# One state-space stage instead of two: tables loaded during the scan, leaving products moved ahead of a last chunk

## What is computed

```python
def _ssm_mixer(hn, ...):
    proj = hn @ w_in                      # 1024 -> 2048
    u, z = proj[..., :SSM_WIDTH], proj[..., SSM_WIDTH:]
    ug = u.reshape(bsz, s, 64, 16)        # 64 groups of 16 channels, 64 complex states each
    y_fwd = _ssm_direction(ug, ...)       # h[t] = abar * h[t-1] + bb @ u[t];  y[t] = Re(c @ h[t])
    y_bwd = flip(_ssm_direction(flip(ug), ...))
    y = y_fwd + y_bwd + d * u
    gl = jax.nn.gelu(y)
    y = gl * jax.nn.sigmoid(gl @ w_glu + b_glu) * jax.nn.silu(z)
    return y @ w_out
```

## Time and profile before

| | us |
|---|---|
| three runs | 2629.58, 2631.95, 2637.1 (median 2631.95) |
| profiled execution | 2628.88 |
| its span, first to last instruction | 2627.0 |
| PE busy | 2325.1 (89%) |
| VectorE busy | 1185.6 (45%) |

### The profile page before, as it was taken

One profiled execution on the slowest core, in us unless ns is written; L12 is line 12 of the kernel. 1 busy time (PEld: TensorE's weight loads), 2 busy tenths in 40 slices (PEclk: granted clock), 3 DMA queues, 4 the chain that ended last, 5 costly groups with the idle time before them and its releaser, 6 DMA issues. The chain is left out here.

```text
span 2627.0 us, 38336 instructions
## 1 busy us (share of the span) xinstructions
PE 2325.1 (89%) x13896; PEld 1865.8 (71%) x13896; DVE 1185.6 (45%) x2668; ACT 886.2 (34%) x2256; POOL 841.2 (32%) x1283
## 2 busy tenths in 40 slices
PE   4999999999999999999999999398799980558888
PEld 3777777777777777777777777277788760457767
DVE  5242443443353353353353353343325999435434
ACT  4233434333433433333333333232433210133221
POOL 1715655555565465466111111010111110211200
PEclk9999999999999999999999999599899995778989
DMA  4212221322222222222221220254554420874333
GB/s 143 60 51 61 60 80 51 84 74 56 74 67 73 66 75 73 66 83 65 64 63 45 47 63 21 65 185 155 202 169 150 144 93 0 213 208 154 136 138 120
DMA packets 191828, 249.69 MB, mean 95 GB/s; under 512 B 86176, under 2 KB 140320, under 8 KB 189472
## 3 DMA queue, kind: packets, MB, share of 16 engines
q1 hardware_dynamic: 191648, 247.30, 31.8%
HBM read 153.23 MB, written 62.55 MB: 82 GB/s over the span
## 5 line engine op out<-in xcount | busy, mean ns | idle before, releaser
L1066 PE MATMUL att_pj<-hT_hi,att_wh 128*128 128x512 f32 (+1 forms) x1920 | 710.0, 370 | 10.8 <-DVE att_wl L848 10.8
L1066 PE MATMUL att_pj<-hT_hi,att_wl 128*128 128x512 f32 (+1 forms) x1920 | 683.8, 356 | 0.0
L1066 PE MATMUL att_pj<-hT_lo,att_wh 128*128 128x512 f32 (+1 forms) x1920 | 682.7, 356 | 0.0
L704 POOL TENSOR_TENSOR att_sw<-att_sw,att_rope 128x1280 f32<-128x1280 f32 x48 | 201.5, 4198 | 762.9 <-DMA att_sw<-att_t 762.8
L1066 PEld LDWEIGHTS att_pj<-hT_hi,att_wh 128*128 128x128 f32 x1920 | 364.5, 190 | 58.5 <-DVE att_wl L848 11.4
L860 DVE CUSTOM_DVE_ANT_0 att_sm<-att_sc,att_mask 128x128 f32<-128x128 f32 (+2 forms) x480 | 152.4, 355 | 561.6 <-PE att_sc L982 560.4
L1066 PEld LDWEIGHTS att_pj<-hT_hi,att_wl 128*128 128x128 f32 x1920 | 363.6, 189 | 53.0
L1066 PEld LDWEIGHTS att_pj<-hT_lo,att_wh 128*128 128x128 f32 x1920 | 364.9, 190 | 45.5
L730 ACT ACTIVATE att_pr<-att_sm,att_stats 128x128 f32<-128x128 f32 (+2 forms) x480 | 215.0, 449 | 434.1 <-PE att_tr L992 313.0
L772 ACT COPY att_t<-att_pj 128x512 f32<-128x512 f32 (+1 forms) x216 | 111.3, 515 | 377.9 <-PE att_pj L1066 377.7
L879 DVE TENSOR_TENSOR att_t<-att_t,att_rope 128x1280 f32<-128x1280 f32 x48 | 71.8, 1495 | 201.8 <-DMA att_sw<-att_t 201.8
(11 more groups left out here) (224 smaller groups left out, 3835.7 us busy)
## 6 DMA issues: line engine op xcount, KB each, us to landing
att_raw<-in_w_att_dram SPq DMA_DIRECT2D x80, 512.0 KB, 3.8
att_sw<-att_t SPq DMA_DIRECT2D x192, 160.0 KB, 2.9
f_scratch<-att_ft SPq DMA_DIRECT2D x32, 256.0 KB, 2.3
e_scratch<-att_place SPq DMA_DIRECT2D x8, 1024.0 KB, 4.6
front_raw<-in_w_ssm_dram SPq DMA_DIRECT2D x16, 512.0 KB, 6.4
front_f<-f_scratch SPq DMA_DIRECT2D x16, 512.0 KB, 5.1
front_f<-e_scratch SPq DMA_DIRECT2D x16, 512.0 KB, 3.6
back_e<-e_scratch SPq DMA_DIRECT2D x8, 1024.0 KB, 7.5
```

The source lines that it names most:

```text
L704: pool.tensor_tensor(sw[:], sw[:], rope[:, 1], ALU.mult).then_inc(sin_done, 1)
L1066: last = pe.matmul(pj[:, c % 3, 0:n], w[:, k % 2, kt], h[:, kt, lo:lo + n], start=(r == 0), stop=(r == CHUNK_MMS - 1))
```

## The change

Front and back become one block, `ssm_stage`. The projection's tiles (`hh`, `hl`, `raw`, `wh`, `wl`, f) give their memory to `e` (seven of eight batches), `near` (all taps), `u2` and `yb`, so the loads of these wait for the last projection product (`done` at 3*NT) and no longer for the end of the scan. PE makes the local products of the first 8 of 24 joints (a joint is 3, 3 or 2 groups of a batch) as soon as they are loaded, into all 8 PSUM banks; after the scan the entering products of joint after joint follow, with the local products of a later joint between them. ACT takes over the forward entering copies from POOL and applies gelu to a whole joint. `states` has no extra column for the zero state (160 instead of 162 columns a row), the scan takes 127 steps (31 for both sequences, 96 for the prompt), and the first column is cleared by DVE ahead of it. In the front part the leaving products of batch n-1 and ACT's copies of them (one instruction a group) go ahead of the third chunk of tile n, and no longer behind it.

```diff
@@ SP
+            sp.wait_ge(k_stored, 16 * HALVES)
+            sp.wait_ge(done, 3 * NT)
+            near_load(0)
+            u_again(0)
+            u_again(1)
+            for b in range(2):
+                e_load(b)
+            near_load(1)
+            near_load(2)
+            for b in range(2, E_BUFS):
+                e_load(b)
+            sp.wait_ge(stored, U_STORED)
+            u_again(2)
+            u_again(3)
+            for b in range(NB):
+                if b + 4 < NB:
+                    u_again(b + 4)
+                sp.wait_ge(y_out, PARTS * (b + 1))
+                for t in range(L):
+                    sp.dma_start(y_scratch[b, :, t].rearrange("(g c) n -> c g n", c=SC),
+                                 yb[t * SC:(t + 1) * SC, b % 2]).then_inc(y_stored[b % 2], 16)
+                if b + E_BUFS < NB:
+                    e_load(b + E_BUFS)
@@ ACT
                 for c, (lo, cnt) in enumerate(CHUNKS):
+                    if c == len(CHUNKS) - 1 and 1 <= n <= NB:
+                        for g in range(GB * (n - 1), GB * n):
+                            act.wait_ge(left, g + 1)
+                            act.copy(states[0:64, g, :, 1:NC], part(g, slice(0, 64))[:, :, 0:NC - 1]).then_inc(fwd, 1)
                     act.wait_ge(done, 3 * n + c + 1)
...
+            def entering(j):
+                if j >= 2:
+                    act.wait_ge(y_done, j - 1)
+                g = joint_groups(j)
+                act.copy(en[0:64, j % 2, 0:len(g)], states[0:64, g[0]:g[-1] + 1]).then_inc(enter_f, 1)
...
+            act.wait_ge(step, 4 * STEPS_ALL + 1)
+            entering(0)
+            entering(1)
+            for j in range(JOINTS):
+                b, g = j // PARTS, joint_groups(j)
+                act.wait_ge(y_done, j + 1)
+                if b >= 2 and j % PARTS == 0:
+                    act.wait_ge(y_stored[b % 2], 16 * L * (b // 2))
+                act.activation(yb[:, b % 2, g[0] % GB:g[-1] % GB + 1],
+                               py[:, j % BANKS, 0:len(g) * NC].rearrange("p (g n) -> p g n", n=NC),
+                               ACT.Gelu_apprx_tanh).then_inc(y_out, 1)
+                if j + 2 < JOINTS:
+                    entering(j + 2)
@@ DVE
-                prev = st[:, :, :, bass.ds(c, n, step=PC + 1)]
-                cur = st[:, :, :, bass.ds(c + 1, n, step=PC + 1)]
+                prev = st[:, :, :, bass.ds(c, n, step=PC)]
+                cur = st[:, :, :, bass.ds(c + 1, n, step=PC)]
...
-            with dve.Fori(0, SCH // TURN) as q:
+            with dve.Fori(0, STEPS_BOTH // TURN) as q:
                 for j in range(TURN):
                     scan_step(TURN * q + j, 2)
+            for c in range(STEPS_BOTH // TURN * TURN, STEPS_BOTH):
+                scan_step(c, 2)
@@ PE
                 for c, (lo, cnt) in enumerate(CHUNKS):
+                    if c == len(CHUNKS) - 1 and 1 <= n <= NB:
+                        leaving(n - 1)
...
-                if 1 <= n <= NB:
-                    leaving(n - 1)
...
+            pe.wait_ge(out, 3 * NT)
+            pe.wait_ge(k_out, 2 * HALVES)
+            for j in range(BANKS):
+                near_part(j)
+            for j in range(JOINTS):
...
+                pe.wait_ge(enter_f, j + 1)
+                pe.wait_ge(enter_b, 2 * (j + 1))
...
+                last.then_inc(y_done, 1)
+                if j >= 1 and j - 1 + BANKS < JOINTS:
+                    pe.wait_ge(y_out, j)
+                    near_part(j - 1 + BANKS)
```

## The result

| | before | after |
|---|---|---|
| median of the runs, us | 2632.44 | 2601.31 |
| lowest to highest, us | 2629.58 to 2637.10 | 2600.31 to 2608.68 |
| profiled execution, us | 2628.88 | 2602.16 |
| its span, us | 2627.0 | 2600.3 |
| waits of PE for u ahead of the leaving products, us | none | 10.7, in 8 waits |

The ratio is 0.9886, interval 0.9863 to 0.9909: 1.1% faster. Four runs of each stand behind it.

A forecast was written before the change was run, and what follows sets the result against it. An end-to-end chain of projection with leaving products, scan and back stage was taken as the bound. From 2628.9 us, -35.3 + 10.7 - 2.3 gave 2602; 3 us more for a median made 2605, range 2588 to 2620.

The forecast's parts named there:

- the three large steps: Against the profiled 2628.9 us: back stage after the scan -35.3, front part ahead of the scan +10.7, scan -2.3; sum 2602.
- Behind the scan: Scan's end to the next stage: 57.4 us in place of 92.7, a gain of 35.3 (30 to 37).
- 46.2 + 1.7 + 1 + 1: Back stage, us: PE's entering and local products 46.2, clock 1.7, ACT in the last joints 1, waits for stores 1.
- the lower clock: Back stage: PE, idle ahead of the scan's end, starts at 1.2 GHz before going to 2.4, costing 1.7 us.
- the waits that I had given 2 us: Back stage: ACT about tied with PE in the last joints, 1 us (0 to 3); gelu waiting for stores, 1 (0 to 4).
- lockstep: Rival, back stage: copy, gelu and products of a joint follow each other; +25 us at worst, half likelier: 2617; chance 0.09.
- lasting lower clock: Rival, back stage: PE stays at 1.2 GHz through the joints, 46.2 us become 92, total 2650; chance 0.04.
- Leaving products ahead: Front part: PE waits 1.7 us for u in 8 batches, 13.6; one third chunk given back, -2.87; net +10.7 us.
- The scan: Scan on VectorE: one step of both sequences gone, 2.32 us; slowing by loads beside it taken as 0.
- The pitch: Scan: rows of `states` at 640 instead of 648 bytes, costed at nothing.
- The rival that a pitch of 640 bytes makes elements dearer: Scan instructions: 126 us hang on it; from 25 us slower than before, at half 2668; chance 0.04.
- The loads: Taps, u and e moved behind the last projection product: 12.8 MB at 245 GB/s, 52 us, hidden in PE's 98 us idle.

## Why the prediction was right, step by step

The forecast was 2605 us, the median is 2601.3, and the signs and sizes of the three large steps hold. On the profiled executions: +11.6 ahead of the scan (10.7 predicted), -3.2 in it (-2.3), -35.2 behind it (-35.3). Together -26.8; the spans differ by 26.7. The sum of the prediction was 2602 for a profiled execution, and 2602.16 was measured. This is closer than the terms deserve: the front part cost 0.9 us more than foreseen, and the scan gave 0.9 more. The 3.7 us between forecast and median come from the 3 us added to get from an execution to a median: after the change the median lies 0.9 us below the profiled execution.

**Behind the scan**, 57.5 us against 57.4 predicted. The same kernel's second profile has 58.9 us here, and those of the kernels that change only the front part 56.6 to 57.6, so agreement to 1 us is what the profiles can show. The first entering product comes 1.2 us after the scan (1.1). From there to PE's end, 2254.11 to 2303.95, is 49.8 us, where I had 46.2 + 1.7 + 1 + 1 = 49.9. Inside, the terms shifted: the lower clock cost 5.99 - 3.42 = 2.6 us and not 1.7, while the waits that I had given 2 us came to the 0.49 for an entering copy at 2299.37; none is for the stores of y. The last gelu at 2303.99 and the stores take 6.45 us (6.4). Rivals: no lockstep, since PE is busy 49.3 of 57.5 us; no lasting lower clock, since the stretch has a granted clock of 0.92. That the early loads are the cause is shown by holding them back (112.6 us), and the share of the early local products by holding those back (65.1).

**Leaving products ahead.** The mechanism is shown by four runs: put back, 11 us are gained; in the kernel before alone, 9 are lost; with u landing 1.8 us sooner, the waits end; made only for the last batch, the front part is 2.9 us shorter than with none ahead. The term itself was not as I had it: 8 waits of 1.7 us were foreseen, 13.6, and they sum to 10.7, 1.34 each. The landing is as foreseen (median 5.7 us), but the load is issued on average 5.65 us after its batch's first store, where it was 6.01 before: three of the eight took 6.5, 6.5 and 7.3 us then, one takes 6.5 now. This is about the 0.36 us that each wait fell short; why these few are longer is not shown. Two things that I had not costed fill the gap. PE's period from the first to the second batch, with a wait of 1.04 us, is 1.28 us longer than before (19.43 against 18.15), so a restart costs 0.24 beyond its wait; the other periods give the same 0.24 or 0.25, 1.9 for eight. And the batch behind the longest wait, 2.08 us, ran 6.29 us instead of 4.61, at a lower granted clock. The stretches are the first 4.6 us of the first, third and seventh batch:

```profile
1880.07:1884.67 4.60, 4.60 (x34) 4.60 (x35) 3.67 (x14) 2.92 (x7) 0.00 (x0) 1.00 0.02 6
1919.98:1924.58 4.60, 4.60 (x22) 4.60 (x23) 2.32 (x9) 1.76 (x5) 0.00 (x0) 0.64 0.04 14
2000.12:2004.72 4.60, 4.59 (x34) 4.60 (x35) 3.75 (x14) 2.92 (x7) 0.00 (x0) 1.00 0.01 4
```

10.7 + 1.9 + 1.7 - 2.87 = 11.4 of the 11.6 measured; the total was near by errors that offset each other, which is luck. In the kernel before with the reordering alone, where no batch ran slow, 10.0 + 1.9 - 2.87 = 9.0 of 9.1.

**The scan.** One double step less was 2.3 us by my sum; with the old pitch it is 1.7 us (230.6 to 228.85). The pitch, costed at nothing, gives another 1.4: the step that fell short here is the one that let the pitch count for nothing. The rival that a pitch of 640 bytes makes elements dearer holds for the double steps alone, 1.7 us, where it needed 25.

**The loads.** At 245 GB/s I estimated 52 us. They took 65, from 2174.89 until the last u that the first eight joints need had landed. Two errors make the difference. I had counted 12.8 MB, with 1.3 for the four loads of u; they are 640 KB each, 2.6 MB, so the sum is 14.2 MB and the estimate 58 us. The issues from 2174.8 to 2241 show it (count, KB each, median us to landing):

```profile
ssm_e<-e_scratch SPq DMA_DIRECT2D x7, 1024.0 KB, 14.6
ssm_near<-kernel_scratch SPq DMA_DIRECT2D x16, 192.0 KB, 12.9
ssm_u<-u_scratch SPq DMA_DIRECT2D x4, 640.0 KB, 15.5
ssm_near<-kernel_scratch SPq DMA_DIRECT2D x8, 128.0 KB, 8.9
```

And the estimate averaged over kinds that differ nearly fourfold: the taps ran at 114 GB/s with the engines full (share 1.28), e and u at 415. By these rates 4.2 MB of taps and 10.0 of e and u make 61 us. The 197 GB/s in my expectation for the late loads is 12.8 MB over 65 us and is wrong with them. The error cost nothing, because the cover held 78 us, from 2174.89 to the scan's end. The margin was 12.7 us. The same average misled my expectation for the loads held until the scan's end, 2618 us against 2653 measured: the taps stand ahead of the first product there, at the slow pace.

## What to carry to other kernels

Before work is moved ahead on the engine that sets the pace, add up the age of its input at the new place, from the producer's end to the landing; if it is late there, look first at what the queue carries just ahead of that input, since reordering two issues gave back here what the move had cost. Make a move that pays once (a last chunk behind the last batch) for the last batch only. Count the bytes of moved loads issue by issue, cost them by the pace of their own kind of piece, and write down the margin of the work that hides them: here a miscount and a mean over kinds together were off by 13 us, and the margin was 12.7.

## What I had not expected of the hardware

- Loads of 512-byte pieces over 16 partitions ran at 114 GB/s with all DMA engines busy, contiguous ones over 128 partitions at 415 GB/s in the same kernel. Whether the length of the piece or the number of partitions makes it was not tried.
- With rows of 640 in place of 648 bytes, a scan step of 128 elements a partition became cheaper (144.0 against 147.1 us for 96) and one of 256 dearer (83.5 against 81.8 for 31). All eleven profiles agree; why the two go apart is open.
- The granted clock fell behind one of the eight waits of PE in the front part. In the changed kernel it was 0.64 of full, so partly at 1.2 GHz, behind the wait of 2.08 us, and the batch took 6.29 us in place of 4.61. Other profiles have the same 6.29 us behind waits of 1.93 us (the changed kernel again), 1.84 (rows of 648 bytes), 2.22 and 3.01 (late loads), each time in the third batch. Behind waits of 1.84 us in the changed kernel and 1.97 in the kernel before with the reordering, batches took 4.61 us. So the length of the wait does not decide alone, and what else does is open.
